# The odd attention's modulation runs two units later, and one run of the even down product five chunks later

## What is computed

```python
cond = jax.nn.silu(c)
for l in range(2):
    mod = cond @ ada_w[l] + ada_b[l]
    sh1, sc1, g1, sh2, sc2, g2 = [m[:, None, :] for m in jnp.split(mod, 6, axis=-1)]
    h = _rms_norm(x, norm_mix[l]) * (1.0 + sc1) + sh1
    y = _even_mixer(h, ...) if l % 2 == 0 else _odd_mixer(h, ...)
    x = x + g1 * (y @ w_out[l])
    h = _rms_norm(x, norm_ffn[l]) * (1.0 + sc2) + sh2
    x = x + g2 * ((jax.nn.silu(h @ wg) * (h @ wu)) @ wd)
```

## Time and profile before

| | us |
|---|---|
| median of 3 runs (lowest, highest) | 1469.69 (1468.08, 1469.96) |
| the profiled execution | 1468.73 |
| its span in the trace | 1467.0 |
| PE busy (share of the span) | 1191.2 (81%) |
| VectorE busy | 615.8 (42%) |
| ScalarE busy | 475.6 (32%) |
| DMA, share of the chain that ended last | 22% |

### The profile page before, as it was taken

One profiled execution on the slowest core, in us unless ns is written; L12 is line 12 of the kernel. 1 busy time (PEld: TensorE's weight loads), 2 busy tenths in 40 slices (PEclk: granted clock), 3 DMA queues, 4 the chain that ended last, 5 costly groups with the idle time before them and its releaser, 6 DMA issues.

```text
span 1467.0 us, 19464 instructions
## 1 busy us (share of the span) xinstructions
PE 1191.2 (81%) x7703; PEld 874.9 (60%) x7703; DVE 615.8 (42%) x1240; ACT 475.6 (32%) x767; POOL 7.6 (1%) x54
## 2 busy tenths in 40 slices
PE   5888888575676756846897888999999978999998
PEld 4665565242332323413675438899898735999986
DVE  3473652010010000101663676655535656565553
ACT  4561621000000000002532335555433447455541
POOL 1000000000000000000000000000000000000000
PEclk9897888798888878978897678899999988999999
DMA  8542149999999999999446431865546472655520
GB/s 294 173 150 80 59 168 424 430 429 430 431 429 428 431 430 428 431 425 401 164 152 244 172 116 58 264 204 203 191 151 223 174 274 70 222 181 187 205 98 29
DMA packets 121729, 368.67 MB, mean 251 GB/s; under 512 B 9842, under 2 KB 56093, under 8 KB 110878
## 3 DMA queue, kind: packets, MB, share of 16 engines
q1 hardware_dynamic: 120556, 367.26, 65.1%
q10 hardware_dynamic: 1074, 0.08, 0.1%
HBM read 366.28 MB, written 1.05 MB: 250 GB/s over the span
## 4 chain that ended last, share of the span: by engine, by line
PE 57%; DMA 22%; DVE 12%; ACT 5%; issue 3%; SPq 1%; DVEq 0%; ACTq 0%
PE ps L1826 54%; DMA more<-in_w_gate_dram 8%; DMA more<-in_w_down_dram 7%; DMA more<-in_w_up_dram 6%; PE ps L1830 3%; DVE st L32 3%; DVE ring_r L32 2%; DVE R_c L32 2%; SPq L669 1%; DVE X_c L32 1%; DVE R_a L32 1%; DVE X_a L32 1%; ACT W_c_r L32 1%; ACT X_c L32 1%; DVE sc L32 1%
## 5 line engine op out<-in xcount | busy, mean ns | idle before, releaser
L1826 PE MATMUL ps<-hT_r,ring_r 128*128 128x256 f32 x864 | 243.7, 282 | 0.0
L1826 PE MATMUL ps<-ring,xg 128*32 128x512 f32 x640 | 140.1, 734 | 126.1 <-DMA more<-in_w_gate_dram 79.3
L1826 PEld LDWEIGHTS ps<-ring,xg 128*32 128x32 f32 x640 | 36.9, 132 | 222.3 <-issue 222.3
L1826 PEld LDWEIGHTS ps<-hT_r,ring_r 128*128 128x128 f32 x864 | 166.0, 192 | 0.0
L32 DVE TENSOR_TENSOR ring_r<-ring,W_c_r 128x1024 fp32r<-128x1024 f32 x94 | 115.2, 1225 | 96.3 <-ACT W_c_r L32 92.4
L1826 PE MATMUL ps<-R_c_r,W_c_r 128*128 128x256 f32 x608 | 152.7, 283 | 0.0
L32 DVE TENSOR_TENSOR ring_r<-ring,X_c_r 128x1024 fp32r<-128x1024 f32 x88 | 107.8, 1225 | 95.2 <-ACT X_c_r L32 92.3
L1826 PE MATMUL ps<-R_c_r,X_c_r 128*128 128x256 f32 x576 | 147.7, 284 | 0.0
L1826 PE MATMUL ps<-more,xg 128*32 128x512 f32 x384 | 134.6, 726 | 0.0
L32 ACT ACTIVATE W_c_r<-ring 128x1024 fp32r<-128x1024 f32 x94 | 99.7, 1060 | 87.3 <-PE ps L1826 83.0
L32 ACT ACTIVATE X_c_r<-ring 128x1024 fp32r<-128x1024 f32 x88 | 93.3, 1061 | 89.6 <-PE ps L1826 84.4
(11 more groups left out here) (280 smaller groups left out, 1912.4 us busy)
## 6 DMA issues: line engine op xcount, KB each, us to landing
ring<-in_ada_w_dram SPq DMA_DIRECT2D x24, 2048.0 KB, 8.1
ring<-in_w_gate_dram SPq DMA_DIRECT2D x20, 2048.0 KB, 18.9
ring<-in_w_up_dram SPq DMA_DIRECT2D x20, 2048.0 KB, 20.0
ring<-in_w_down_dram SPq DMA_DIRECT2D x20, 2048.0 KB, 19.4
more<-in_w_gate_dram SPq DMA_DIRECT2D x12, 2048.0 KB, 27.9
more<-in_w_up_dram SPq DMA_DIRECT2D x12, 2048.0 KB, 28.4
more<-in_w_down_dram SPq DMA_DIRECT2D x12, 2048.0 KB, 27.9
ring<-in_ffn_gate_dram SPq DMA_DIRECT2D x22, 1024.0 KB, 5.9
```

What stands on the lines that cost most here:

```text
L1826: return pe.matmul(out, lhsT, rhs, start=start, stop=stop, skip_group_check=True)
```

## The change

Two numbers of the plan and two points change. In the odd attention pieces 17 to 23 have their runs at units 2, 4, ..., 14 where they stood at 0, 2, ..., 12, and the last close is at unit 15. The output projection's loads stay at unit 8, so they now come ahead of three pieces where they came ahead of two. In the down product piece 15 keeps the place of its load, but its run is ahead of the begin of chunk 11 (was 6) and its close ahead of chunk 14 (was 9).

```diff
@@ Plan.ffn
             for q in range(min(4, 22 - 4 * u)):
                 if run is not None and 4 * u + q == run:
-                    self.ada(("f", len(self.chunks)))
-                if run is not None and 4 * u + q == run + 3:
-                    self.close(("f", len(self.chunks)))
+                    self.ada(("f", len(self.chunks) + 5))
+                    self.close(("f", len(self.chunks) + 8))
                 self.feed(k, q)
@@ make_plan
-    p.units(4, 16, (0, 2, 4, 6, 8, 10, 12), 8, 2)
+    p.units(4, 16, (2, 4, 6, 8, 10, 12, 14), 8, 2)
```

## The result

| | us |
|---|---|
| after: median of 22 runs (lowest, highest) | 1476.33 (1473.27, 1488.34) |
| before: median of 22 runs beside them | 1469.64 (1467.73, 1478.29) |
| ratio after to before, 95% interval | 1.0042 (1.0026 to 1.0058) |
| profiled execution of after, its span | 1488.34, 1486.6 |

The kernel is slower, by 6.7 us from median to median; the forecast was 1474.3, in a range of 1471.3 to 1477.8. The profiled execution of after happens to be its longest. The even FFN's first product starts at 939.4 us in it, at 928.8 in before's, and no instruction up to there was changed: 10.6 us of the difference of the spans are there already. So I compare stretches between two fixed points of the program, not starts.

A forecast was written before the change was run, and what follows sets the result against it. PE was taken as the bound, except where it waits for VectorE, whose chunk 151 decides when x is updated. Terms -1.4 - 0.8 + 6.8 = +4.6 us on a 1467.0 span, plus 1.73 and 0.96, gave 1474.3 us; range 1471.3 to 1477.8.

The forecast's parts named there:

- the span that the forecast gave itself: Whole kernel: the main forecast's own interval, 1472.7 to 1476 us, with a chance of 0.62.
- rival 2: Behind the output projection: PE's idling adds one or two low-clock dips of 1.7 us; 1476.0 to 1477.7, chance 0.18.
- Down product, -1.4: Down product: PE's wait ahead of the later run shrinks, saving 1.4 us; bounds 0 to 3.1 saved.
- Begin of the attention, -2.4: Odd attention's begin: first run 3.1 us earlier, less 0.7 for the clock, net -2.4 at unit 4.
- The 0.7: Behind the attention's first run: loss taken for the clock staying low, between nothing and 1.7 us.
- Units 4 to 16, -1.1 and +3.1: Odd attention: one `gates` close fewer before unit 14 saves 1.1; run and close in pair 14 and 15 cost 3.1.
- Tail, -0.4: Attention's end, before the output projection: PE's shorter wait for VectorE saves 0.4 us, between 0 and 1.97.
- Attention in all: Odd attention up to the output projection's begin: -0.8 us, bounds +0.8 and -3.
- 2.2 were forecast: Output projection's begin: 2.2 us earlier than before, at 1237.6 instead of 1239.84.
- the sign of being wrong that the prediction names: Output projection: its beginning later than before would show the prediction wrong.
- The load, +6.8: Behind the output projection: gu 0 waits for chunk 143's buffer, delaying `add_xT` by 6.8 us, fully on the path.

The follow-up runs named there:

- the one where it was filled: Changed kernel with the output projection's loads at unit 10, plus unused matmuls ahead of the odd attention's unit 2 and the down product's run: 1467.13 us, ratio 0.9967.
- attention alone: Kernel before with only the odd attention's runs moved to units 2 to 14, down product as before: 1480.61 us, ratio 1.0065.
- late load alone: Kernel before with only the output projection's loads moved from unit 8 to 6, so gu 0 is loaded late: 1481.3 us, ratio 1.0079.
- both of after: The changed kernel, timed and traced in two sittings: 1476.33 us, ratio 1.0042, and 1477.56 us, ratio 1.0040.
- both with loads at unit 10: Changed kernel with the output projection's loads at unit 10 instead of 8, in two sittings: 1465.38 us, ratio 0.9979, and 1466.9 us, ratio 0.9965.
- the attention's fill: Changed kernel with the output projection's loads at unit 10, plus 14 unused matmuls ahead of the odd attention's unit 2: 1468.35 us, ratio 0.9968.
- down alone: Kernel before with only piece 15's run and close five chunks later in the down product: 1467.42 us, ratio 0.9987.
- filled sums: Changed kernel plus 14 unused matmuls on PE between the output projection and the odd FFN's sums: 1474.75 us, ratio 1.0023.
- the two with runs side by side: Changed kernel with attention runs at units 2, 3, 4, 6, 8, 10, 12: 1470.45 us; the same with piece 15's close seven chunks later: 1468.2 us.

## Why the prediction was right, and which terms were not

The sign, the place and the chain were right: a load that was 41 us early became the last thing that the FFN waits for. The median of 1476.33 lies in the range. It does not lie in the span that the forecast gave itself (1472.7 to 1476) but, just, in that of rival 2 (1476.0 to 1477.7), and rival 2's mechanism took part. That the number came within 2.0 us is in part luck, as the sum at the end of this section shows. By its steps:

**Down product, -1.4: right as a wait, the clock open.** The wait fell from 3.37 to 1.97 in every trace with the new place, the one where it was filled aside. Whether the clock then falls differs. In the three traces with the old place (before, attention alone, late load alone) it fell each time. With the new place and no fill it fell in five (both of after, both with loads at unit 10, the attention's fill) and stayed up in four (down alone, filled sums, and the two with runs side by side). Those five have A between 205.5 and 208.0, the four between 202.9 and 204.2; before has 205.7. In the five, and in no other, the sums ahead of the odd projections also ran in part at the lower clock, 4.23 to 4.64 us where they otherwise take 3.63. So A is 1.5 to 2.8 us shorter than before where the clock stayed up, and from 0.2 shorter to 2.4 longer where it fell; only the medians average this: -2.4 for this half alone where -1.4 was forecast, with an interval that includes zero.

**Begin of the attention, -2.4: the charge for the clock was wrong.** The turns of unit 4 stand 19.7 us behind the first scores; before, 22.7 (1194.98 - 1172.27). That is -3.0: the run ended at 1201.4 and nothing behind it was slow. In the other trace of the same kernel it is 18.7, -4.0. The 0.7 that I took between 0 and 1.7 was not there.

**Units 4 to 16, -1.1 and +3.1: right.** Turns of unit 4 to turns of unit 14 took 30.1 us (1203.37 to 1233.50), as worked out, and the pair 14 and 15 took 6.92. At unit 16 this sums to -1.1 instead of -0.4.

**Tail, -0.4: none.** From those turns to the output projection it is 9.7 us, 9.8 before. PE's wait for VectorE did fall by 1.0 (0.94 for 1.97), but the units behind took it back, half of it as a longer wait for ScalarE (0.73 for 0.23 us), the engine that the prediction had named. Attention in all: -1.1 in this trace, -2.6 in the other one of the same kernel, against -0.8. Counted from the even FFN's first product the projection begins 0.3 us earlier than before in this trace and 1.9 in the other one, where 2.2 were forecast; that it begins later by the clock of the span (1250.13) is the 10.6 us ahead of all this, not the sign of being wrong that the prediction names.

**The load, +6.8: the term that was mis-sized.** The buffer came free 14.4 us behind the projection's begin instead of 13.6; the first 12 us of this stretch had a clock of 0.74, before's 0.82. The halves landed 5.6 and 8.0 us after their issues as taken from before, and `add_xT` came 29.7 behind, against 28.9 forecast. But "fully on the path, since PE has nothing between the projection and the sums" was wrong on both sides. In before the sums did not wait for `add_xT`: they started at 1264.58, 2.6 us behind it, when PE ended its last projection chunk. After, they start 1.1 us behind it. So PE's own work had covered 1.5 us, and the sums moved by 6.0 (24.7 to 30.7 behind the projection's begin), not by 7.5. And then they took 6.96 instead of 3.63 us: +3.3. Together +9.3, where I had 6.8. Rival 2 had the cause, one or two dips at 1.7 us each, but looked for them in the FFN's products. They were in 16 float32 matmuls of one column ahead of these, which I had counted as cover for the clock ("turns and sums come between"). The medians give this term 10.8 to 11.9.

**The sum.** Taken by medians, the early gains are -4.1 to -4.4 (change without the late load) and the load is +10.8 to +11.9. That is where +6.7 comes from, against -2.2 and +6.8 forecast: both sides were too small, by some 2 and 4 to 5 us, and the errors partly cancel. The direction and the mechanism are owed to the reasoning; a miss of only 2.0 us is owed to this. Of the early gains the traces show 1.1 us in the attention and 2.8 in the down product where its clock stays up; the traced executions with the loads at unit 10 took 1471.89 and 1470.59, well above their medians, and their A is not shorter than before's. Eight of the twelve executions of the first took 1463.5 to 1465.4, so its trace shows one of the slower. That the faster executions are those in which that clock stays up would fit, but only one execution of each was traced, and it is not shown; the down product alone has A at 202.9 in a trace that is itself slower than its median.

## What to carry to other kernels

When work is moved past a load in the plan, look first at whose buffer each following load now inherits. Here small gains of 4 us together were paid with 11 us, and moving the loads by one more piece kept the gain and avoided the price. When a wait is put ahead of a matrix engine, price the work behind it at the lower clock, even if it is only 16 float32 matmuls of one column. And work taken away from a stretch where PE waits is not won if it has to be made in a stretch where PE is full: it gains only where it lands in another wait.

## What the runs showed of the hardware that I had not expected

- 16 float32 matmuls of one column (x32 in the trace) take 3.63 us at 2.4 GHz and 6.96 at 1.2: so short a free size pays a factor of 1.9 as well. The stretch from 1276 to 1294 had a mean clock of 0.62, although PE was busy for 12.78 of its 18 us.
- A wait of 1.97 us in an otherwise full stretch was followed by the lower clock in five traces and not in four, with the same instructions around it.
- PE makes one and the same chunk of 24 matmuls of 256 columns in 2.72 or in 2.85 us (113 or 119 ns each) at a granted clock of 1.00, in two executions of one program. No cause was found.
- The transfer of gu 0, on idle queues, had both halves in 8.4 us after the first issue. A load of the down product, 2 MB in one transfer, has a median of 7.9 us (ten of them in the same trace). The Trainium skill (DMA: Bandwidth & Descriptors, Anatomy of one DMA), in a fit for single transfers that GpSimd issues, gives an estimate of 6.8 us for 2 MB; for these transfers from SyncE the trace does not agree, and the measurement decides.
